# A rebuilt prologue in a two-layer decoder kernel: memory transposed into four banks, x read from PSUM, loads reordered

## What is computed

```python
def memory_branch(q_mem, mem, norm_mem, w_mem_kv):
    k_m, v_m = jnp.split(rmsnorm(mem, norm_mem) @ w_mem_kv, 2, axis=-1)
...
def self_decoder_layer(x, mem, norm_attn, w_in, ...):      # layer A
    proj = rmsnorm(x, norm_attn) @ w_in
    q_sb, k_sb, v_sb, q_mem = jnp.split(proj, [SB_WIDTH, 2 * SB_WIDTH, 3 * SB_WIDTH], axis=-1)
    o_mem = memory_branch(q_mem, mem, norm_mem, w_mem_kv)
    x = x + jnp.concatenate([o_sb, o_mem], axis=-1) @ w_out
    return x + conv_ffn(rmsnorm(x, norm_ffn), ffn_up, ffn_conv, ffn_down)
```

## Time and profile before

| | us |
|---|---|
| median of 3 runs | 1265.68 (1265.61, 1265.68, 1267.77) |
| the profiled execution, its own time | 1265.73 |
| its span in the trace | 1263.9 |
| PE busy in the span | 1214.4 (96%) |

### The profile page before, as it was taken

The page is one execution under the profiler, slowest core; times in us unless marked ns, Lnnn a source line. Parts: engine busy times, 40 slices in busy tenths (PEclk is TensorE's granted clock), DMA queues, the critical chain, the costliest instruction groups (busy, mean ns, idle before and its releaser), DMA issues.

```text
span 1263.9 us, 16994 instructions
## 1 busy us (share of the span) xinstructions
PE 1214.4 (96%) x5975; PEld 997.0 (79%) x5975; DVE 808.7 (64%) x1251; ACT 554.9 (44%) x918; POOL 100.7 (8%) x133
## 2 busy tenths in 40 slices
PE   4899999999999999999999999889999999999998
PEld 4777887787788888878887877778788888888886
DVE  4866666667777777752246766776777777774226
ACT  5545665644444444432245543534444444442222
POOL 0200333333000000000012000001200000000000
PEclk9999999999999999999999999999999999999999
DMA  7421211112333333322241222122233333333552
GB/s 233 124 62 52 66 51 43 59 50 80 89 99 89 94 100 100 100 91 92 100 150 34 58 76 67 51 67 68 83 100 100 93 91 99 100 102 102 133 140 73
DMA packets 175701, 112.51 MB, mean 89 GB/s; under 512 B 20062, under 2 KB 167838, under 8 KB 175646
## 3 DMA queue, kind: packets, MB, share of 16 engines
q1 hardware_dynamic: 175646, 111.79, 29.5%
HBM read 107.58 MB, written 2.10 MB: 87 GB/s over the span
## 4 chain that ended last, share of the span: by engine, by line
PE 76%; DVE 12%; issue 6%; ACT 4%; POOL 2%; DMA 1%; DVEq 0%; SPq 0%; POOLq 0%; ACTq 0%
PE bank L1364 16%; PE bank L1366 15%; PE bank L1365 15%; PE bank L1678 8%; PE bank L1651 8%; DVE w_lo L896 2%; PE bank L1664 2%; DVE y_lo L902 2%; PE bank L1691 2%; ACT w_hi L587 1%; PE bank L1458 1%; POOL ar L567 1%; PE bank L1479 1%; DVE af L1236 1%; POOL ar L545 1%
## 5 line engine op out<-in xcount | busy, mean ns | idle before, releaser
L1364 PE MATMUL bank<-y_hi,w_hi 128*128 128x512 f32 x928 | 366.5, 395 | 8.4 <-DVEq L1036 3.9
L1366 PE MATMUL bank<-y_hi,w_lo 128*128 128x512 f32 x928 | 361.8, 390 | 0.0
L1365 PE MATMUL bank<-y_lo,w_hi 128*128 128x512 f32 x928 | 361.6, 390 | 0.0
L896 DVE TENSOR_TENSOR w_lo<-raw,w_hi 128x1024 fp32r<-128x1024 f32 x188 | 232.3, 1236 | 158.7 <-ACT w_hi L587 155.4
L587 ACT ACTIVATE w_hi<-raw 128x1024 fp32r<-128x1024 f32 x186 | 196.3, 1055 | 283.5 <-PE bank L1366 136.8
L1364 PEld LDWEIGHTS bank<-y_hi,w_hi 128*128 128x128 f32 x928 | 174.5, 188 | 49.5 <-issue 9.7
L1365 PEld LDWEIGHTS bank<-y_lo,w_hi 128*128 128x128 f32 x928 | 174.5, 188 | 36.4 <-issue 1.2
L1366 PEld LDWEIGHTS bank<-y_hi,w_lo 128*128 128x128 f32 x928 | 174.3, 188 | 36.5
L1651 PE MATMUL bank<-ar,w_hi 128*128 (+1 forms) x288 | 88.8, 389 | 0.8 <-DVE af L1128 0.8
L756 ACT ACTIVATE af<-af,conv 128x512 f32<-128x512 f32 x88 | 63.0, 716 | 35.8 <-DVE af L1128 35.8
L1678 PE MATMUL bank<-w_hi,ar 128*128 128x512 f32 x288 | 77.1, 390 | 0.8 <-DVE af L1128 0.8
(11 more groups left out here) (200 smaller groups left out, 1617.6 us busy)
## 6 DMA issues: line engine op xcount, KB each, us to landing
raw<-in_a_ffn_up SPq DMA_DIRECT2D x44, 512.0 KB, 3.7
raw<-in_b_ffn_up SPq DMA_DIRECT2D x44, 512.0 KB, 3.7
raw<-in_a_ffn_down SPq DMA_DIRECT2D x22, 512.0 KB, 3.2
raw<-in_b_ffn_down SPq DMA_DIRECT2D x22, 512.0 KB, 3.6
raw<-in_a_w_in SPq DMA_DIRECT2D x20, 512.0 KB, 3.7
raw<-in_w_kv_shared SPq DMA_DIRECT2D x12, 512.0 KB, 3.8
raw<-in_a_w_out SPq DMA_DIRECT2D x8, 512.0 KB, 3.4
raw<-in_b_w_in SPq DMA_DIRECT2D x8, 512.0 KB, 3.9
```

The lines of the kernel that those rows point to most:

```text
L896: nc.vector.tensor_tensor(w_lo[:, m % SPLIT, :], raw[:, m % RAW, :], w_hi[:, m % SPLIT, :].bitcast(F32), ALU.subtract).then_inc(lo_done, 1)
L1364: mm(bank, w[0], y[0][:, k, :], start=(k == 0), stop=False)
L1365: mm(bank, w[0], y[1][:, k, :], start=False, stop=False)
L1366: last = mm(bank, w[1], y[0][:, k, :], start=False, stop=(k == KT - 1))
```

## The change

- Loads: `cs` is split, and only its first 128 KB (identity and the column of -1) comes first; the memory comes in two DMAs of 512 KB, each with a semaphore of its own; x comes in two DMAs of 1 MB (left and right columns). `cst_nat` and the rest of `cs` are issued behind weight 2. The seven gains and the two tap loads are issued by ACT, ahead of its table load.
- Gains and taps are transposed into bank 5 in place of bank 7.
- Memory: all 16 transposes go at once into half-banks of banks 2, 3, 6 and 7, with no wait between them. The splits go in the order YM: first the eight slices for layer A (k = 0, 2, 1, 3, 4, 6, 5, 7), then four for layer B; the last four are made within tiles 0 and 1. In one bank ACT's next read waits for DVE's last (`ym_lo`). `ring(1)` moves into the middle. Tile 0 takes its slices in the order YM.
- x: `y_hi` and `y_lo` are made from the PSUM bank (`high_x`, `x_tile`), and then DVE copies the slice to `hT`; the square is made from `hT` later (`square_x`). An x bank is released after all three.
- `cr` is copied in the pass n = 3 of the tile loop; `x_tile(6)` waits for it.
- Tile 8 is cut: three slices, the last V transpose, five slices. The last V split comes ahead of `ring(10)`.

```diff
@@ sync
-            sp.dma_start(cs[:], cst[:, CS_FROM:C_ALL]).then_inc(ld_cst, 16)
-            sp.dma_start(cst_nat, cst[:, 0:C_R]).then_inc(ld_cst, 16)
-            sp.dma_start(m_nat, mem[0].rearrange("(t p) d -> p t d", p=P)).then_inc(ld_mem, 16)
...
+            sp.dma_start(cs[:, 0:2 * P], cst[:, CS_FROM:CS_FROM + 2 * P]).then_inc(ld_id, 16)
+            for t in range(2):
+                sp.dma_start(m_nat[:, t, :], mem[0, P * t:P * (t + 1), :]).then_inc(ld_mem[t], 16)
...
                 if n == 2:
-                    sp.dma_start(x_nat, x[0].rearrange("(t p) d -> p t d", p=P)).then_inc(ld_x, 16)
+                    for hf in range(2):
+                        sp.dma_start(x_nat[:, :, half(hf)],
+                                     x[0, :, half(hf)].rearrange("(t p) d -> p t d", p=P)).then_inc(ld_x[hf], 16)
+                if n == 3:
+                    sp.dma_start(cst_nat, cst[:, 0:C_R]).then_inc(ld_cst, 16)
+                    sp.dma_start(cs[:, 2 * P:C_ALL - CS_FROM], cst[:, CS_FROM + 2 * P:C_ALL]).then_inc(ld_cst, 16)
@@ scalar
+            def high_x(k):
+                act.wait_ge(x_tr, k + 1)
+                nc.scalar.activation(y_hi[:, k, :], banks[4 + k % 2][:], ACT.Copy, scale=gain(G_A, k)).then_inc(yhi, 1)
+            def square_x(k):
+                act.wait_ge(h_ready, k + 1)
...
+            def mem_high(i):
+                l, k = i // KT, YM[i]
+                act.wait_ge(m_tr, k // 2 + 1)
+                same_bank = [j for j in range(i) if YM[j] // 2 == k // 2]
+                if same_bank:
+                    act.wait_ge(ym_lo, same_bank[-1] + 1)
...
             ring(0)
+            for i in range(12):
+                mem_high(i)
+                if i == 3:
+                    ring(1)
             for n in range(8):
+                if n:
+                    high_x(n)
                 ring(n + 2)
...
-                absorb(0, n)
+                if n == 0:
+                    high_x(0)
+                square_x(n)
+                if n < 2:
+                    mem_high(2 * n + 12)
+                    mem_high(2 * n + 13)
@@ vector
             ring(0)
+            for i in range(12):
+                mem_low(i)
+                if i == 5:
                     ring(1)
             def x_tile(n):
-                dve.wait_ge(x_tr, n + 1)
+                dve.wait_ge(yhi, n + 1)
+                nc.vector.scalar_tensor_tensor(out=y_lo[:, n, :], in0=banks[4 + n % 2][:], scalar=gain(G_A, n),
+                                               in1=y_hi[:, n, :].bitcast(F32), op0=ALU.mult,
+                                               op1=ALU.subtract).then_inc(ylo, 1)
...
                 nc.vector.tensor_copy(hT[:, n, :], banks[4 + n % 2][:]).then_inc(h_ready, 1)
...
+            mem_v_low(3)
             ring(N_QMA + 2)
-            mem_v_low(3)
@@ tensor
             for k in range(KT):
-                if k >= 3:
-                    pe.wait_ge(ym_lo, 2 * (k - 2))
                 for t in range(2):
+                    last = nc.tensor.transpose(MT[k][:, P * t:P * (t + 1)], m_nat[:, t, P * k:P * (k + 1)], ident)
+                if k % 2:
+                    last.then_inc(m_tr, 1)
...
-            tile(N_QMA, N_QMA, 0, y, lambda k: pe.wait_ge(ylo, y_wait(0, k)))
+            steps(N_QMA, N_QMA, range(0, 3), y, lambda k: pe.wait_ge(ylo, y_wait(0, k)))
             v_transpose(3, 2)
+            steps(N_QMA, N_QMA, range(3, KT), y, lambda k: pe.wait_ge(ylo, y_wait(0, k)))
             sum_squares(0)
```

More of the change, by code:

```diff
@@ L164, in build @@
         m_nat = hT[:, 0:4, :].rearrange("p k t -> p (k t)").rearrange("p (t d) -> p t d", t=2)
-        m_junk = hT[:, 4:8, :].rearrange("p k t -> p (k t)").rearrange("p (t d) -> p t d", t=2)
+        m_junk = [sq[:].rearrange("p b t -> p (b t)"), hT[:, 4:6, :].rearrange("p k t -> p (k t)")]
+        TAB = banks[5]
+        MT = [(banks[2], banks[3], OB, TR)[k // 2][:, M * (k % 2):M * (k % 2) + M] for k in range(KT)]
+        YM = [0, 2, 1, 3, 4, 6, 5, 7] + [4, 6, 5, 7, 0, 2, 1, 3]
         qkf = af[:, 0:512]
@@ L198, in build @@
         newt = sq[:, 1, :]
-        ld_cst, ld_mem, ld_x, ld_g, ld_cw = (sem(n) for n in ("ld_cst", "ld_mem", "ld_x", "ld_g", "ld_cw"))
+        ld_id, ld_cst, ld_g, ld_cw = (sem(n) for n in ("ld_id", "ld_cst", "ld_g", "ld_cw"))
+        ld_mem = [sem(f"ld_mem_rows{t}") for t in range(2)]
+        ld_x = [sem(f"ld_x_cols{hf}") for hf in range(2)]
         raw_full = [sem(f"raw_full{i}") for i in range(RAW)]
@@ L627, in _ @@
             act.wait_ge(tab_tr, 1)
-            link(nc.scalar.activation(gains[:], TR[:, 0:56], ACT.Copy))
-            nc.scalar.activation(conv[:], TR[:, 64:64 + 264], ACT.Copy).then_inc(tab_ready, 1)
-            ring(0)
[L631 to L636, removed]
+            link(nc.scalar.activation(gains[:], TAB[:, 0:56], ACT.Copy))
+            nc.scalar.activation(conv[:], TAB[:, 64:64 + 264], ACT.Copy).then_inc(tab_ready, 1)
+            def mem_high(i):
[4 more added lines that the diff above has]
+                    act.wait_ge(ym_lo, same_bank[-1] + 1)
+                nc.scalar.activation(ym[:, l, 0, k, :], MT[k], ACT.Copy, scale=gain((G_MA, G_MB)[l], k)).then_inc(ym_hi, 1)
+            ring(0)
+            for i in range(12):
+                mem_high(i)
+                if i == 3:
+                    ring(1)
             def mem_v_high(iv):
@@ L648, in _ @@
                     mem_v_high(mem_value(n - 1))
-                absorb(0, n)
+                if n == 0:
[4 more added lines that the diff above has]
+                    mem_high(2 * n + 13)
+                if n == 3:
+                    act.wait_ge(ld_cst, 32)
+                    nc.scalar.activation(cr[:], cst_nat, ACT.Copy).then_inc(cr_ready, 1)
             def mem_exp(i):
@@ L979, in _ @@
                 if n == 0:
-                    dve.wait_ge(m_tr, KT)
                     x_tile(0)
-                absorb_low(0, n)
+                if n < 2:
+                    mem_low(2 * n + 12)
+                    mem_low(2 * n + 13)
             def qk_float(i, n, scale, l=0, residues=False):
@@ L1390, in _ @@
                     o = 64 + (3 * l + t) * 2 * FT
-                    last = nc.tensor.transpose(TR[:, o:o + 2 * FT], nat[0:2 * FT, P * t:P * (t + 1)],
+                    last = nc.tensor.transpose(TAB[:, o:o + 2 * FT], nat[0:2 * FT, P * t:P * (t + 1)],
                                                ident[0:2 * FT, 0:2 * FT])
@@ L1395, in _ @@
             for k in range(KT):
-                if k >= 3:
-                    pe.wait_ge(ym_lo, 2 * (k - 2))
                 for t in range(2):
-                    last = nc.tensor.transpose(YM_BANK[k % 3][:, P * t:P * (t + 1)], m_nat[:, t, P * k:P * (k + 1)], ident)
-                last.then_inc(m_tr, 1)
+                    last = nc.tensor.transpose(MT[k][:, P * t:P * (t + 1)], m_nat[:, t, P * k:P * (k + 1)], ident)
+                if k % 2:
+                    last.then_inc(m_tr, 1)
             def v_transpose(iv, count):
@@ L1407, in v_transpose @@
                     pe.wait_ge(v_lo, iv)
+                if iv == 0:
+                    pe.wait_ge(ym_lo, KT + 4)
                 for t in range(count):
@@ L1420, in x_transposes @@
             def x_transposes(n):
-                pe.wait_ge(ld_x, 16)
+                pe.wait_ge(ld_x[n // 4], 16)
                 if n >= 2:
@@ L1434, in ready @@
                     if n == 0:
-                        pe.wait_ge(ym_lo, 2 * k + 2)
+                        pe.wait_ge(ym_lo, YM.index(k) + 1)
+                    if n == 4 and k == 0:
+                        pe.wait_ge(ym_lo, 2 * KT)
                 l = n // 4
-                tile(n, n, 0, (ym[:, l, 0], ym[:, l, 1]), ready, M)
+                pe.wait_ge(lo_done, n + 1)
+                if n >= 2:
+                    pe.wait_ge(evicted, n - 1)
+                steps(n, n, range(KT) if n else YM[0:KT], (ym[:, l, 0], ym[:, l, 1]), ready, M)
                 if n in (3, 4, 7):
```

48 lines of the change are left out of this document (24 added, 24 removed).

## The result

The kernel after takes 1259.8 us in the median of 6 runs (1258.33 to 1260.31), the kernel before on the same chip 1266.53 (6 runs, 1264.83 to 1268.31): a ratio of 0.9944 [0.9932, 0.9957], 6.7 us by the medians, where 9.8 were forecast. The profiled execution took 1258.79 (before: 1265.73), 6.9 us less, and its first memory scores start at 66.34, 7.2 us before those of the earlier trace rows.

What follows compares the result with a forecast made beforehand. PE, working 96% of the span, was taken as the bound, with all gains ahead of the first scores: 6.9 - 1.2 + 3.2 + 0.9 = 9.8 us, so 1265.7 to 1255.9; range 1254.5 to 1258, with rivals 1251 to 1261.

Steps and rivals of the forecast that it cites:

- The start up to the transposes: Startup: fewer bytes ahead let memory transposes begin at 11.3 in place of 15.14, 3.8 us earlier; taps come in time.
- T0: Mark at the end of tile 0: forecast at 19.4 us against 26.3, 6.9 us earlier.
- ACT's issues: Startup: nine load issues, 3.6 us, plus the table load keep ACT busy until near 5.8 us.
- Transposes and splits: Up to tile 0's end: 16 memory transposes take about 3.9 us, splits alternate between ACT and DVE; tile 0 ends at 19.4.
- The loop: Tiles 1 to 7: 26.7 us where it took 25.5, giving back 1.2, with waits ahead of tiles 2 and 3.
- `y_lo` from PSUM: Tile loop: DVE's `y_lo` takes about 0.7 us beside POOL's additions, where it averaged 1.55.
- Tile 8: Tile 7's end to the sum of squares: 6.8 us for 10.0, the 2.67 wait gone, 3.2 us won.
- The sum's clock: Sum of squares before the first scores: with PE busy up to it, 1.02 us for 2.05; 0.9 us won.
- the port conflict: Rival, chance 0.10: in the tile loop POOL's additions slow `w_lo` in place of `y_lo`; 3.5 us back, 1259.5.
- start-bound rival: Rival, chance 0.12: startup bound by DMA or issue, memory at 9 or later or weights late; 2 to 4 us back, 1259.
- Serial passes: Rival, chance 0.04: longer hold of x banks makes loop passes 4.8 us for 3.3; 10.5 us lost, 1266.4.
- PE paced throughout: Rival, chance 0.15: DVE is never late in the tile loop; 2.6 us better, 1253.3.

Runs made afterwards that it cites:

- e1: Kernel after, with only the gains transposed ahead of the memory; the taps are transposed behind it and copied within the splits; ratio 0.9922 to the kernel before.
- e4: Kernel after, with the nine small loads issued by SP behind the memory and ahead of weight 0, not by ACT; ratio 0.9914 to the kernel before.
- e10: e4 with x's high part, low part and copy ahead of `ring(2)` in pass 0 too; ratio 0.9916 to the kernel before.
- e5: Kernel after, with the memory again slice by slice through three banks, both layers together, `ring(1)` ahead, tile 0 in natural order; ratio 0.9968 to the kernel before.
- e8: Kernel after, with the loop pass in the old order and `y_hi`, `y_lo` read from `hT`; ratio 0.9974 to the kernel before.
- e9: Kernel after, with the loop pass in the old order but `y_hi`, `y_lo` read from the PSUM bank; ratio 0.9963 to the kernel before.
- e2: Kernel after, with `y_hi` and `y_lo` made from `hT` after the copy, rest of the pass in its new order; ratio 0.9985 to the kernel before.
- e11: e10 with `ring(1)` behind all eight layer A splits and two more layer B splits within the tiles; median 1254.79 us, ratio 0.9905 to the kernel before.
- e12: Kernel before, with only the cut of tile 8 and the last V split ahead of `ring(10)`; ratio 0.9989 to the kernel before.

## Why the prediction was right, and where it was off

- **The direction and the range held**; the size was short by 3 us (6.7 to 6.9 for 9.8).
- **The start up to the transposes: the step that failed.** "They come in time by any rate but that one, whose cost would be under 1 us", said of the taps. They came at that one: 6.88 us after their issue, as slowly as before. The rate used for the memory was right: its halves, issued at 1.2 and 1.7, took 4.3 and 5.3 us, so the second had landed by 7.0, forecast 7.1 (what set the scaling, at 11.41 for 11.3, was ACT's queue: its squares run at 6.18 and 7.24 without a wait). The price was wrong too, as I had put the taps beside the chain; but they gate the gains, the gains gate `ring(0)` on ACT and all splits, and T0 follows them one to one. T0 was forecast at 19.4 and came at 21.55, by its end; e1, without the wait for the taps, has it 1.92 us sooner. With the taps in time (e4) the marks are T0 18.6, scores 63.57, against a forecast of 63.7, and the ratio is 0.9914: the other terms were sound. That e4 meets the 63.7 so closely is in part luck, as its first memory transpose came at 10.38 for a forecast of 11.3; with e10's arrival it would be near 64.7.
- **ACT's issues** (until 5.8 forecast) cost what was said, the first square at 6.18; that it need not have been paid at all is what e4 adds.
- **Transposes and splits.** 3.67 us for 3.9; PE waits for DVE's low parts twice in tile 0, 0.39 and 0.91 us. In e4 T0 is 8.22 us behind the first transpose; forecast were 8.1 (11.3 to 19.4).
- **The loop**: 26.93 for 26.7, with its two waits. The bound "24.1 with DVE and ACT never late" was reached by no kernel: e5 comes nearest with 24.92, of which 0.58 is waiting.
- **`y_lo` from PSUM**: 0.74 for 0.7, and 2.1 us by e8 and e9.
- **Tile 8**: the total held (-3.05 for -3.2), its reason by half. "3.2 us won" was put down to the cut; 1.5 are the cut's and 1.6 come from `y_lo`. **The sum's clock** held in size (0.88 for 0.9), not as an effect of the wait alone.
- **The rivals.** What the rival calls the port conflict (the traces show longer rows, not a port) did move to `w_lo`, but not its price: `w_lo` keeps 1.22 us and POOL's addition, which starts second, grows to 1.52 to 1.81 in six of seven, off the path. The start-bound rival was half of what happened: small loads in ACT's queue beside the large ones, not the memory. Serial passes came only in e2. PE paced throughout came in none, with e5 and e10 nearest.

## What to carry to other kernels

Put small loads that gate a chain right behind the first large load and ahead of the bulk of the weights (here this and the move to the same queue were made together, and only the two together are shown); and a wait should cover only what its followers need (gains, not taps). Before a wait is credited with a gain, follow the engine behind it: here a new wait took part of its place, and a shorter operation two steps earlier supplied the rest. When an operation's time hangs on its operand's place and on what another engine does beside it (here `y_lo` beside POOL's addition, 1.79 from SBUF and 0.74 from PSUM), price it by a pair of kernels that differ in as little else as can be, as the order of a pass changes who meets whom.

## What the runs showed of the hardware that I had not expected

- **In these rows the operation that began second took longer.** DVE and POOL in the kernel after:
```profile
33.11 1.22 DVE L929 TENSOR_TENSOR w_lo<-raw,w_hi 128x1024 fp32r<-128x1024 f32 x1
...
33.94 1.52 POOL L532 TENSOR_TENSOR ss<-ss,sq 128x512 f32<-128x512 f32 x1 [1.98 <-ACT sq L610]
```
  `w_lo`, begun first, takes 1.22 us, for 1.23 where no addition is beside it (at 23.51), and the addition is 0.23 longer than its 1.29 of the earlier trace rows. Where the addition begins first it takes 1.28, and `y_lo` from `hT` 1.79 (e8, at 34.38) for 0.75 with no addition beside it (e8, at 26.05). In e8 `y_lo` ends 0.54 to 0.56 us behind the addition whether it began 0.02 or 0.37 after it (1.46 to 1.81 long), and in the kernel after an addition that began 0.39 us or more before the end of `w_lo` ends 1.12 to 1.15 behind it (1.52 to 1.81 long); the one that began 0.12 before it, at 40.76, takes 1.30. By differences of these rows the second was 1.04 us longer where 1.24 of the first were left (e8, at 34.38) and 0.52 longer where 0.67 were left (kernel after, at 47.04). What holds it back isn't shown. With `y_lo` from PSUM neither is longer: 0.74 and 1.29 (e9, above).
- **The same load, two queues**: PE could use it 7.0 us after its issue on ACT's queue, 3.3 after that on SP's (e4), with fewer large loads beside it, as above.
- **Tile 0 at a slower pace.** In the kernel after, matmuls of 256 columns start every 0.21 us in the first part of tile 0 (16.28 to 17.34) and every 0.12 behind it, while the granted clock reads 1.00 throughout. In e10 and e11 there is no such part. In e12 the slower pace lasts nearly to the end of tile 0, to 27.0 us:
```profile
26.79 0.41 PE L1366 MATMUL bank<-ar,w_lo 128*128 128x256 f32 x1
27.00 0.32 PE L1364 MATMUL bank<-ar,w_hi 128*128 128x256 f32 x1
```
  In the kernel before, with the same work up to there, it ended by 24.2, and T0 was 26.10 for 27.39. Why it lasted longer stays open. In e5 it holds for 17 of tile 0's 24 matmuls, so some of e5's later T0 is this pace and not the order of the memory.
